# Loading query tiles and keys of a head pair with one transfer instead of two, with queries stored twice in scratch

## The reference

```python
n = rms_norm(x, g_mix)
q, k, v, xr, gr, gates = jnp.split(n @ w_in, SPLITS, axis=-1)
q = q.reshape(b, t, N_KV_HEADS, GROUP, HEAD_DIM)      # 4 key heads, 4 query heads for each, 64 wide
k = k.reshape(b, t, N_KV_HEADS, HEAD_DIM)

def stick_breaking_weights(z, mask):
    log_keep = jnp.where(mask, jax.nn.log_sigmoid(-z), 0.0)
    later = jnp.concatenate([log_keep[..., 1:], jnp.zeros_like(log_keep[..., :1])], axis=-1)
    tail = lax.cumsum(later, axis=z.ndim - 1, reverse=True)
    return jnp.where(mask, jnp.exp(jax.nn.log_sigmoid(z) + tail), 0.0)

# attend_prompt, for each block of queries
z = jnp.einsum('bqhgd,bshd->bhgqs', qb, kp) * SB_SCALE + bias_f
w = stick_breaking_weights(z, mask)                    # keys before the query only
return jnp.einsum('bhgqs,bshd->bqhgd', w, vp)

# attend_sample does the same for one new token of 8 sequences against 2048 cached keys,
# which lie in 16 pages of 128 tokens each, found through page_table
x = x + (gate_a * attn + gate_b * rnn) @ w_out
up, ffn_buf_new = causal_dwconv(rms_norm(x, g_ffn) @ w_up, ffn_buf, w_ffn_conv, b_ffn_conv)
x = x + (jax.nn.gelu(ua) * ub) @ w_down
```

## Time and profile before

| | us |
|---|---|
| median of 3 runs | 2058.79 (2057.93 to 2062.34) |
| the profiled execution | 2064.17 |
| its span, first to last instruction | 2062.5 |
| busy in the span: PE | 1899.3 (92%) |
| busy: DVE, ACT, POOL | 1211.0, 929.6, 199.2 |
| mean granted clock of PE | 0.961 of full speed |
| load of a query tile half, line 778 | 272 transfers, 32 KB each |
| load of a key range half, line 784 | 24 transfers, 64 to 100 KB |
| store of a query head, line 221 | 16 transfers, 260 KB each |
| bytes read from and written to DRAM | 124.31 MB, 17.61 MB |

### The profile page before, as it was taken

One profiled execution on the slowest core, in us unless ns is written; L12 is line 12 of the kernel. 1 busy time (PEld: TensorE's weight loads), 2 busy tenths in 40 slices (PEclk: granted clock), 3 DMA queues, 4 the chain that ended last, 5 costly groups with the idle time before them and its releaser, 6 DMA issues. The chain is left out here.

```text
span 2062.5 us, 38464 instructions
## 1 busy us (share of the span) xinstructions
PE 1899.3 (92%) x14580; PEld 1732.3 (84%) x14580; DVE 1211.0 (59%) x1999; ACT 929.6 (45%) x1506; POOL 199.2 (10%) x98
## 2 busy tenths in 40 slices
PE   6998999989998999898996978999999999999985
PEld 5897878878787878786873768999999999999984
DVE  6101667767685858576776344755665566556655
ACT  5121677776767686768764222222222122212213
POOL 0121000000000000000000003221122112211210
PEclk9999999999999999999997988999999999999998
DMA  3334213131314232332223211211111111101104
GB/s 133 109 87 112 75 47 101 42 105 44 97 44 107 56 85 66 80 83 71 74 58 95 93 62 50 62 51 31 51 51 51 31 51 51 51 31 51 51 10 181
DMA packets 198685, 143.47 MB, mean 70 GB/s; under 512 B 58289, under 2 KB 187890, under 8 KB 198528
## 3 DMA queue, kind: packets, MB, share of 16 engines
q1 hardware_dynamic: 198554, 141.73, 23.9%
HBM read 124.31 MB, written 17.61 MB: 69 GB/s over the span
## 5 line engine op out<-in xcount | busy, mean ns | idle before, releaser
L87 PE MATMUL d_p_up<-n_hi,d_w_hi 128*128 128x346 f32 x1056 | 341.9, 324 | 14.7 <-POOL d_w_lo L1762 7.9
L87 PE MATMUL d_p_up<-n_hi,d_w_lo 128*128 128x346 f32 x1056 | 341.3, 323 | 0.0
L87 PE MATMUL d_p_up<-n_lo,d_w_hi 128*128 128x346 f32 x1056 | 341.0, 323 | 0.0
L1910 DVE TENSOR_TENSOR mix<-mix,d_p_down 128x346 f32<-128x346 f32 x264 | 136.1, 515 | 267.8 <-PE d_p_down L1959 267.8
L87 PE MATMUL b_p_proj<-n_hi,b_w_hi 128*128 128x350 f32 x768 | 264.4, 344 | 15.9 <-DVE b_w_lo L1117 9.4
L1762 POOL TENSOR_TENSOR d_w_lo<-w_raw,d_w_hi 128x1024 fp32r<-128x1024 f32 x45 | 109.1, 2426 | 1483.0 <-ACT d_w_hi L1793 1483.0
L87 PE MATMUL b_p_proj<-n_lo,b_w_hi 128*128 128x350 f32 x768 | 251.4, 327 | 0.0
L87 PE MATMUL b_p_proj<-n_hi,b_w_lo 128*128 128x350 f32 x768 | 251.3, 327 | 0.0
L1807 ACT ACTIVATE d_up<-d_p_up 128x346 f32<-128x346 f32 x132 | 60.1, 457 | 399.6 <-PE d_p_up L87 399.6
L87 PEld LDWEIGHTS d_p_up<-n_hi,d_w_hi 128*128 128x128 f32 x1056 | 200.4, 190 | 16.0 <-POOL d_w_lo L1762 8.3
L87 PEld LDWEIGHTS d_p_up<-n_lo,d_w_hi 128*128 128x128 f32 x1056 | 200.8, 190 | 0.0
(11 more groups left out here) (262 smaller groups left out, 3849.4 us busy)
## 6 DMA issues: line engine op xcount, KB each, us to landing
w_raw<-in_w_in SPq DMA_DIRECT2D x45, 512.0 KB, 4.2
w_raw<-in_w_up SPq DMA_DIRECT2D x45, 512.0 KB, 3.7
b_page<-in_cache_k SPq DMA_DIRECT2D x128, 128.0 KB, 2.1
b_page<-in_cache_v SPq DMA_DIRECT2D x128, 128.0 KB, 2.1
w_raw<-in_w_down SPq DMA_DIRECT2D x22, 512.0 KB, 3.4
b_q_in<-q_scr SPq DMA_DIRECT2D x272, 32.0 KB, 2.2
mix<-in_x_prompt SPq DMA_DIRECT2D x8, 512.0 KB, 7.9
w_raw<-in_w_out SPq DMA_DIRECT2D x8, 512.0 KB, 3.5
```

What stands on the lines that cost most here:

```text
L87: last = pe.matmul(out, w[:, k, :], x[:, k, col:col + width], start=(k == 0 and w is w_hi and x is x_hi), stop=(k == KT - 1 and w is w_lo))
L1910: dve.tensor_tensor(to, to, p_down[:, n % 4, 0:FW], ALU.add).then_inc(down_out, 1)
```

## The change

A query tile is now stored in scratch twice, once for each half of the partitions: `q_scr` has the shape (8 pairs, 128 rows, 2 heads, 1040), where rows 0 to 63 and 64 to 127 hold the same. So one load of 128 partitions fills both halves of a query tile. A key range is loaded by one transfer as well, whose source repeats the same 64 rows twice (`to_broadcast`). The counts that the semaphores are waited for are changed to match. Line numbers below 226 are moved by up to two, those of phase_mix by one.

```diff
--- before.py
+++ after.py
@@ -156,8 +156,8 @@
                     sp.wait_ge(w_lo_ready, index)
                     sp.dma_start(w_raw[:, slot, :, :], w_view[:, :, bass.ds(col, P)]).then_inc(w_in[slot], 16)
 
-                sp.sem_inc(q_stored[0], 32)
-                sp.sem_inc(q_stored[1], 32)
+                sp.sem_inc(q_stored[0], 64)
+                sp.sem_inc(q_stored[1], 64)
                 def load_x(t):
                     if t == 0:
                         sp.dma_start(x_tok[0:DEC, 0, :], g.x_sample.rearrange("s o d -> (s o) d")).then_inc(x_in[0], 16)
@@ -218,8 +218,10 @@
                             sp.dma_start(w_raw[:, 0, :, :], w_view[:, :, XR_COL:XR_COL + P]).then_inc(g.mix_arr[0], 16)
                         sp.wait_ge(q_cols, nth(i, 2, s))
                         for h in range(2):
-                            sp.dma_start(g.q_scr[bass.ds(i * 4 + 2 * s + h, 1), :, :].rearrange("a p c -> p (a c)"),
-                                         q_stage[s][HD * h:HD * (h + 1), FIRST:LAST]).then_inc(q_stored[s], 16)
+                            for half in range(2):
+                                sp.dma_start(g.q_scr[bass.ds(i * 2 + s, 1), HD * half:HD * (half + 1), h, :]
+                                             .rearrange("a p c -> p (a c)"),
+                                             q_stage[s][HD * h:HD * (h + 1), FIRST:LAST]).then_inc(q_stored[s], 16)
 
                 with sp.Fori(0, KT // 2 - 1, 1) as i:
                     q_pair(i, False)
@@ -230,15 +232,15 @@
                     sp.wait_ge(kv_stored[n], 16 * (5 + 3 * 2 if n == 0 else 3 * 2))
                 first.load_v(sp, g, 0)
                 first.load_v_odd(sp, g, 0)
-                sp.wait_ge(q_stored[0], 32 * 2)
+                sp.wait_ge(q_stored[0], 64 * 2)
                 for s in range(2):
                     first.load_q(sp, g, 0, s)
                 q_pair(KT // 2 - 1, True)
                 for n in range(4):
                     sp.wait_ge(kv_stored[n], 16 * (5 + 3 * 2 if n == 0 else 3 * 2))
                 sp.wait_ge(k_stored, 16 * 4)
-                sp.wait_ge(q_stored[0], 32 * 5)
-                sp.wait_ge(q_stored[1], 32 * 5)
+                sp.wait_ge(q_stored[0], 64 * 5)
+                sp.wait_ge(q_stored[1], 64 * 5)
                 sp.wait_ge(old_rows, 32)
                 sp.wait_ge(bias_in, 32)
 
@@ -327,7 +329,7 @@
 
                 def q_pair(i, last):
                     for s in range(2):
-                        act.wait_ge(q_stored[s], nth(i, 32, 31))
+                        act.wait_ge(q_stored[s], nth(i, 64, 63))
                         for c in range(CHUNKS):
                             n = CHUNKS * s + c
                             evacuate(n % 2, nth(i, 6, 12 + n), q_stage[s][:, CW * c:CW * (c + 1)], HD ** -0.5)
@@ -774,16 +776,13 @@
 
     def load_q(self, sp, g, i, s):
         b, q0, nq, nk = unit(s)
-        for half in range(2):
-            sp.dma_start(self.q_in[HD * half:HD * (half + 1), Q_AT[s], :, :],
-                         g.q_scr[bass.ds(i * 2, 2), :, q0:q0 + QB].rearrange("a p c -> p a c"))\
-              .then_inc(self.q_arr[Q_AT[s]], 16)
+        sp.dma_start(self.q_in[:, Q_AT[s], :, :],
+                     g.q_scr[bass.ds(i, 1), :, :, q0:q0 + QB].rearrange("i p a c -> (i p) a c"))\
+          .then_inc(self.q_arr[Q_AT[s]], 16)
 
     def load_k(self, sp, g, group, k0, k1):
-        for half in range(2):
-            sp.dma_start(self.k_in[HD * half:HD * (half + 1), k0:k1],
-                         g.k_scr[bass.ds(group, 1), :, k0:k1].rearrange("a p c -> p (a c)"))\
-              .then_inc(self.k_arr, 16)
+        sp.dma_start(self.k_in[:, k0:k1],
+                     g.k_scr[bass.ds(group, 1), :, k0:k1].to_broadcast([2, HD, k1 - k0])).then_inc(self.k_arr, 16)
 
     def load_v(self, sp, g, group):
         cols = bass.ds(group * HD, HD)
@@ -921,7 +920,7 @@
                         sp.wait_ge(qk_done, nth(i, SLOTS, -1, SLOTS))
                         load_k(group, *K_PARTS[0])
                     else:
-                        sp.sem_inc(k_arr, 96)
+                        sp.sem_inc(k_arr, 48)
 
                 def turn_loads(i, group, fresh, following, first=False):
                     load_q(i, 2)
@@ -1302,9 +1301,9 @@
 
                     b, q0, nq, nk = unit(s)
                     if s == 0:
-                        pe.wait_ge(k_arr, 96 * nth(i, 1, 0))
+                        pe.wait_ge(k_arr, 48 * nth(i, 1, 0))
                     users = q_users(s)
-                    pe.wait_ge(q_arr[Q_AT[s]], 32 * nth(i, len(users), users.index(s)))
+                    pe.wait_ge(q_arr[Q_AT[s]], 16 * nth(i, len(users), users.index(s)))
                     pe.wait_ge(z_copied, nth(i, SLOTS, s))
                     pe.sem_inc(passed, 1)
                     diagonal = nk - min(QB, nk)
@@ -2160,7 +2159,7 @@
         g.h_out = sb("h_out", [P, KT, DEC + 1])
         g.att_dec = sb("att_dec", [P, KT, DEC])
         g.gate_dec = sb("gate_dec", [P, KT, DEC])
-        g.q_scr = nc.dram_tensor("q_scr", (HEADS, HD, PROMPT), F32).ap()
+        g.q_scr = nc.dram_tensor("q_scr", (KT, P, 2, PROMPT), F32).ap()
         g.k_scr = nc.dram_tensor("k_scr", (KVH, HD, PROMPT), F32).ap()
         g.x1_scr = nc.dram_tensor("x1_scr", (HEAD_ROWS + SEQ, D), F32).ap()
         g.v_scr = nc.dram_tensor("v_scr", (PROMPT, KVH * HD), F32).ap()
```

## The result

The changed kernel takes 2068.57 us (median of 9 runs, 2065.07 to 2072.74) against 2062.34 (9 runs, 2057.93 to 2065.52) for the kernel before, measured with it. The ratio is 1.0030 with a 95% interval from 1.0018 to 1.0042: 6.2 us slower (3.7 to 8.7). The prediction was 2061.4 us, between 2053.5 and 2065.5, so the time lies 3.1 us above the end of its range, and not within the 0.2% that it held most likely. Measured again later beside other kernels, the unaltered changed kernel gave 1.0008 (0.9998 to 1.0017), so the size of the loss is less certain than the first interval says. The profiled execution of the changed kernel took 2066.8 us, with a span of 2065.0.

What follows compares the result with a forecast made beforehand. PE, busy 92%, was taken to set the time, with SP's issuing on its chain at three boundaries. +2.0 us (last store) and +0.6 (boundaries) on the 2058.79 median gave 2061.4 us, range 2053.5 to 2065.5.

Steps and rivals of the forecast that it cites:

- What bounds the kernel: Three boundaries to a new group: SP's issuing, page, PE, ACT form the chain; at most 5.9 us to gain.
- Issuing: SP at boundaries to a new group: 0.43 us per query load, 0.35 per key load; pages issued 3.3 us earlier.
- The key load on two engines: Three boundaries: both key ranges on two of 16 DMA engines, page shares queue behind; +0.6 us (-2 to +3).
- The double store: Query stores in phase_qkv: free in the loop, the last store before the barrier adds 2.0 us (1.1 to 2.8).
- First keys at no cost: Three key ranges loaded from 170.2, done by 184, before the last store's issue at 192.55: cost 0.
- The step from the sum to the time: Whole kernel: +2.6 us carried from the runs' median of 2058.79 gives 2061.4 us.
- The size of the sum: Whole kernel: +2.0 us for the last store and +0.6 for the three boundaries, +2.6 us.
- Keys on all engines: Rival: key load spread over all engines, boundaries give their full 5.9 us; -3.9 us, 2054.9; chance 0.27.
- The two engines at 13.3 GB/s: Rival: slower engines, each boundary to a new group costs about 5.5 us more; +18.5 us, about 2077; chance 0.10.
- The change doesn't do what it says: Rival: wide query and key loads cost as much to issue, only the store is left; +2.0, 2060.8; chance 0.05.

Runs made afterwards that it cites:

- e1: Changed kernel with the key load put back to two transfers of 64 partitions, wide queries stored twice kept: 2057.96 us, ratio 0.9978 to the kernel before.
- e4: Changed kernel with keys also stored twice in scratch, so the key load is one plain transfer of 128 rows: 2058.30 us, ratio 0.9979.
- e8: Changed kernel with only the shorter key range of a boundary loaded by broadcast, the longer by two plain loads: 2058.96 us, ratio 0.9977.
- e2: Kernel before with only its two key loads replaced by the one broadcast transfer: 2068.40 us, ratio 1.0032.
- e12: Changed kernel with only the longer key range of a boundary loaded by broadcast, the shorter by two plain loads: 2061.17 us, ratio 0.9983.
- e3: Changed kernel with query and key loads both put back to two transfers, leaving only the double query store: 2066.24 us, ratio 1.0021.
- e6: Kernel before with only SP's wait for the last query stores moved into the first turn of phase_mix: 2064.31 us, ratio 1.0000.
- e7: Kernel before with queries stored once and each tile loaded by one broadcast transfer, keys in two loads: 2065.16 us, ratio 1.0008.

## Why the prediction missed

- **What bounds the kernel: right.** Page, SP, PE, ACT is the chain at the three boundaries. Taking it away (e1, e4, e8) gave the 5.9 us of the earlier trace rows, and 7.5 us in the turns, of which 1.6 stay unexplained.
- **Issuing: the direction right, the size wrong.** A 128-partition load from the doubled scratch costs 539 ns at least and 556 in the middle, not 430; a broadcast key load 600, not 350:

```profile
L779 SPq DMA_DIRECT2D b_q_in<-q_scr x136: 539/556/3152, 183.4 to 1057.1; - x136
...
L784 SPq DMA_DIRECT2D b_k_in<-k_scr x12: 515/600/2563, 171.6 to 851.6; - x12
```

  For the keys that is the upper end, the price of the old shape; for the queries it is 0.13 above the nearest row. A transfer of 128 partitions is not cheap to issue for being wide: the rows that I took, a value load and a page load, have another form. Together 2.64 us are saved in place of 3.3, and 0.9 of it goes again between the last key load and page 14 (2.22 us there in place of 1.32). Why the reading of the page numbers takes longer behind the broadcast load wasn't tested. It cost nothing, since the keys decided.
- **The key load on two engines: right, and shown** by e1, e2, e4, e8 and e12. Its packets run from 409.8 to 417.7 by the trace, 7.9 us for 168 KB, just past the 6.9 to 7.8 forecast. They begin 1.3 us after the issue, not 1.05, and page 14 reaches PE at 418.84, 0.4 past the end of what I gave it. That end, 418.4, was itself 0.3 later than its terms add up to (417.4 + 0.7 = 418.1). The term was mis-sized for another reason too: I compared page 15 with page 15, but when both pages come together PE has the work of both ahead of it (1.86 us, at the low clock). Gaps grew by 0.98, 0.19 and 1.19, +2.4 in place of +0.6, within the -2 to +3 given: the mechanism was right and its price a quarter of what was measured. In the length of the turns it is +1.3.
- **The double store: right in the sum at the first wait, not in its parts.** +2.6 in place of +2.0, within 1.1 to 2.8, and nothing in the loop, as e3 shows. But I had let the bytes set it and given SP's wait of 3.5 us or more as the sign; the wait grew only by 0.5, to 3.0, and issuing by 2.1.
- **First keys at no cost: right in the sum, wrong in the picture.** I had them done by 184 beside SP. In fact SP issued slowly: 5.02 us for three key loads, 2.94 for one value load, and the staging store that stood at 180.53 is issued at 187.85. The cover of 8 us was used up by that, but it held: the last store is issued at 192.11, and e2's first wait is 9.41.
- **The step from the sum to the time: the one that failed.** Measured less forecast is 2068.57 - 2061.4 = 7.2 us. Half of it, 3.6, is the base: I carried +2.6 not to the profiled execution's 2064.17 but to 2058.79, the median of the three runs shown. Measured again the kernel before has 2062.34 (9 runs, those three among them), 2063.85 (35), 2063.65 (32) and 2064.91 (29). The three runs lay 3.5 to 6 us low, and the profiled execution, which lay outside them, was the better level. The same +2.6 on the medians beside which the changed kernel ran gives 2064.9 and 2067.5 for the 2068.57 and 2066.59 measured. The range ended at 2065.5 because every term had bounds and the base had none.
- **The size of the sum: failed too, by the other half.** The step was 6.2 us in place of 2.6. With the base put right, my own range of the forecast (2058.0 to 2064.6) becomes 2061.6 to 2068.2 and still ends below 2068.57. Of these 3.6 us the traces give 0.6 for the last store and 0.7 (turns) to 1.8 (gaps) for the boundaries, the term that I had at +0.6. The remaining 1.2 to 2.3 stay unexplained; the second measurement, +1.7 us (-0.4 to 3.5), doesn't ask for them.
- **Luck.** The two profiled executions, 2064.17 and 2066.8, are 2.6 apart like my sum, and that is chance. The later start of the mix is used up by 214 us, where the clock fell a second time in the kernel before, and when ACT copies the first scores of turn 7 the two are level (973.55 and 973.58). The 2.6 us arise where nothing is changed: from the last product of the output projection (line 1628 of the kernel before) to the last of the feed-forward phase (line 1959) it is 799.7 us in before and in e1, 802.4 and 801.8 in the two profiles of the changed kernel, but also 802.3 in e6, which is the kernel before but for one wait. The clock differs there too: the first products of that phase take 0.49 us in place of 0.32 until 1244.0 us in before and until 1247.3 in the changed kernel.
- **The rivals.** Keys on all engines (0.27) is excluded for this shape and is what e4 built: it gave a ratio of 0.9979, -4.3 us, where I had -3.9. The two engines at 13.3 GB/s (+18.5 us) are excluded: they carried 168 KB in 7.9 us, 21.4 each. "The change doesn't do what it says" is excluded by SP's rows.

## What to carry to other kernels

Replacing two transfers by one saved the issuing engine about half here, but count also over how many DMA engines the one is dealt: a repeat of 2 in front of the source left two, and the pages issued afterwards had a share behind it. Whether that matters is bytes against slack: 66 KB an engine was free here and 168 KB cost more than the whole gain. Storing data twice so that a load becomes plain moves the price to the store: look who waits for the last one, and whether its wait has to stand there. Read a difference of two profiles stretch by stretch before it is believed: here it stood where nothing was changed. And give the base of a prediction a range of its own when only three runs of it are known.

## What was unexpected of the hardware

- SP was slow to issue where two DMA engines had work ahead: it took 5.02 us for three broadcast key loads at 171.59, 2.94 for the one value load after them, and in e7 3.90 in place of 2.46 for loads over all engines behind broadcast ones. That the full engines held it up is an inference; no run sets it apart.
- The granted TensorE clock was lower behind the longer waits of PE at the first boundary: 0.70 and 0.67 of 2.4 GHz from 417 to 420 us behind waits of 2.65 and 5.07, 0.99 behind one of 1.30, with 1.48 us in place of 0.84 for the same scores. Elsewhere nearly equal waits were followed by either level (e1 and e3).
- Whether the clock falls once or twice in the first turn of the mix makes 2.7 us between profiles, whatever the kernel.
- Two measurements of one kernel, with 9 and 11 runs, gave ratios whose 95% intervals don't meet, 1.0018 to 1.0042 and 0.9998 to 1.0017. Part of the spread goes with the clock: of the 96 executions of the kernel before beside e1 to e12, the 25 with a mean granted clock of 0.963 or more took 2060.9 us in the mean, the 23 with 0.959 or less 2065.6. What makes the clock fall more often in one execution stays open, and so does the chip's part: the second measurement ran on the third chip, and the chip of the first is not recorded.
